# Turning x in full 128-column blocks, with router weights in natural row order loaded behind the gated projection

## What is computed

```python
def rms_norm(x, g):
    y = x * rsqrt(mean(x * x, axis=-1) + EPS)
    return y * g

for i in range(2):
    x = x + mixer_i(rms_norm(x, norm_mix_g[i]))
    h = rms_norm(x, norm_ffn_g[i])
    gl = h @ moe_w_router_group[i]       # (1024, 4)
    el = h @ moe_w_router_expert[i]      # (1024, 4, 8)
    # the best group, its two best experts, their weights "combine"
    x = x + sum_e combine_e * ((silu(h @ w_gate_e) * (h @ w_up_e)) @ w_down_e)
return rms_norm(x, final_norm_g)
```

## Time and profile before

| | |
|---|---|
| median of 3 runs | 815.22 us (815.03 to 815.89) |
| profiled execution, its own time | 816.45 us |
| its span | 814.5 us |
| mean granted TensorE clock | 0.947 |
| TensorE busy / weight loads busy | 711.9 us (87%) / 433.9 us (53%) |
| VectorE / ScalarE / GpSimd busy | 307.8 / 239.5 / 48.8 us |
| transfers | 236.33 MB, 290 GB/s over the span |
| chain that ended last | PE 61%, SP's queue 15%, DMA 11%, ACT 6%, DVE 4% |

### The profile page before, as it was taken

One profiled execution on the slowest core, in us unless ns is written; L12 is line 12 of the kernel. 1 busy time (PEld: TensorE's weight loads), 2 busy tenths in 40 slices (PEclk: granted clock), 3 DMA queues, 4 the chain that ended last, 5 costly groups with the idle time before them and its releaser, 6 DMA issues.

```text
span 814.5 us, 16111 instructions
## 1 busy us (share of the span) xinstructions
PE 711.9 (87%) x6350; PEld 433.9 (53%) x6364; DVE 307.8 (38%) x853; ACT 239.5 (29%) x573; POOL 48.8 (6%) x48
## 2 busy tenths in 40 slices
PE   4999699999997686586999998898999999985994
PEld 4889445557555354254444544465655555652552
DVE  6968991144210011010241535527333443332334
ACT  6672802242111011011312223425222342231224
POOL 3594000000000000000000000000000000000000
PEclk9996899999999798898999999999999999997898
DMA  9630507968999999999990573018899961999981
GB/s 255 173 134 2 208 1 313 408 254 324 421 420 419 420 420 420 422 420 409 381 364 5 210 274 135 1 68 346 350 420 420 422 249 39 423 419 420 422 343 53
DMA packets 59055, 236.33 MB, mean 290 GB/s; under 512 B 19104, under 2 KB 19312, under 8 KB 34416
## 3 DMA queue, kind: packets, MB, share of 16 engines
q1 hardware_dynamic: 58096, 235.23, 73.0%
q10 hardware_dynamic: 896, 0.24, 0.1%
HBM read 234.41 MB, written 1.05 MB: 289 GB/s over the span
## 4 chain that ended last, share of the span: by engine, by line
PE 61%; SPq 15%; DMA 11%; ACT 6%; DVE 4%; issue 2%; DVEq 0%; ACTq 0%
PE ps L1885 11%; SPq L433 10%; PE ps L1976 9%; PE ps L1790 7%; PE ps L1940 6%; SPq L431 4%; DMA ring<-in_moe_w_up 4%; PE ps L1865 4%; DMA hT<-in_moe_w_up 3%; DMA work<-in_moe_w_down 3%; PE ps L1905 3%; PE ps L1661 3%; PE ps L1861 2%; PE ps L2039 2%; PE ps L1708 2%
## 5 line engine op out<-in xcount | busy, mean ns | idle before, releaser
L1885 PE MATMUL ps<-ring,work 128*32 128x256 f32 x1440 | 100.4, 405 | 16.9 <-DMA ring<-in_moe_w_up 12.9
L1885 PE MATMUL ps<-work 128*32 128x256 f32 x848 | 87.4, 433 | 20.7 <-DMA work<-in_moe_w_gate 12.5
L1885 PEld LDWEIGHTS ps<-ring,work 128*32 128x32 f32 x1440 | 57.9, 117 | 53.0 <-issue 30.4
L1976 PE MATMUL ps<-ring,hT 128*128 128x512 f32 x192 | 84.8, 594 | 1.2 <-ACT hT L631 1.2
L1401 DVE TENSOR_TENSOR work<-ps,work 128x256 f32<-128x256 f32 x21 | 12.9, 613 | 188.1 <-PE ps L1885 188.1
L1885 PEld LDWEIGHTS ps<-work 128*32 128x32 f32 x848 | 46.9, 124 | 51.4 <-issue 37.6
L1940 PE MATMUL ps<-ring,work 128*32 128x512 f32 x464 | 58.2, 595 | 1.4 <-DMA ring<-in_moe_w_down 1.1
L1976 PEld LDWEIGHTS ps<-ring,hT 128*128 128x128 f32 x192 | 35.6, 190 | 42.1 <-issue 40.5
L1790 PE MATMUL ps<-ring,work 128*128 128x512 f32 x128 | 55.9, 595 | 0.5 <-ACT work L748 0.5
L1885 PE MATMUL ps<-x,work 128*32 128x256 f32 x160 | 43.3, 432 | 6.3 <-DMA ring<-in_moe_w_up 6.3
L1885 PE MATMUL ps<-hT,work 128*32 128x256 f32 x176 | 44.3, 410 | 0.0
(11 more groups left out here) (334 smaller groups left out, 1121.0 us busy)
## 6 DMA issues: line engine op xcount, KB each, us to landing
ring<-in_moe_w_down SPq DMA_DIRECT2D x21, 2048.0 KB, 22.3
ring<-in_moe_w_gate SPq DMA_DIRECT2D x18, 2048.0 KB, 17.5
ring<-in_moe_w_up SPq DMA_DIRECT2D x17, 2048.0 KB, 29.9
work<-in_moe_w_gate SPq DMA_DIRECT2D x10, 2048.0 KB, 30.9
work<-in_moe_w_up SPq DMA_DIRECT2D x9, 2048.0 KB, 20.9
work<-in_moe_w_down SPq DMA_DIRECT2D x9, 2048.0 KB, 25.3
ring<-in_attn_w_qkv SPq DMA_DIRECT2D x6, 2048.0 KB, 20.4
ring<-in_ssm_w_glu SPq DMA_DIRECT2D x4, 2048.0 KB, 8.5
```

The source lines that it names most:

```text
L1885: ins = mm(ps[s, 6 + j // 2, 0:256], xg[:, k, s], pairs[slots[e // 2]][e % 2][:, k, :], start=(k == 0), stop=(k == KD - 1))
L1976: ins = mm(ps[:, qkv_bank(tt, c), :], hT[:, k, tt * P:(tt + 1) * P], win[slot][:, k, :], start=(k == 0), stop=(k == KD - 1))
```

## The change

Block `k` of hT becomes the 128 adjoining columns 128k to 128k + 127, so that a half of a tile is four full blocks of its own PSUM bank. Router weights and the router's gains (`ffg`, a new tile, for both layers) are loaded in that order. The loads stand behind those of the gated projection, and the copies into hT wait for them, as the first logits and the routing do, with 160 in place of 128. `gq` keeps the gains in (q k) order for the gathered rows of the experts.

```diff
@@ -137,6 +137,7 @@
         rb = sb("rb", [P, 2, NG + E])
+        ffg = sb("ffg", [P, 2, KD])
         small = sb("small", [P, 64])
@@ -413,11 +414,6 @@
             for i, g in ((1, a["norm_ffn_g"][0]), (2, a["norm_mix_g"][1]), (3, a["norm_ffn_g"][1])):
                 sp.dma_start(gq[:, i, :], g.rearrange("(k q) -> q k" if i == 2 else "(q k) -> q k", k=KD)).then_inc(s_gains, 16)
-            for l in range(2):
-                sp.dma_start(wr[:, l, :, 0:NG], a["moe_w_router_group"][l].rearrange("(p k) n -> p k n", k=KD)).then_inc(s_router, 16)
-                sp.dma_start(wr[:, l, :, NG:], a["moe_w_router_expert"][l].rearrange("(p k) g e -> p k (g e)", k=KD)).then_inc(s_router, 16)
-                sp.dma_start(rb[:, l, 0:NG], a["moe_b_router_group"][l].partition_broadcast(P)).then_inc(s_router, 16)
-                sp.dma_start(rb[:, l, NG:], a["moe_b_router_expert"][l].rearrange("g e -> (g e)").partition_broadcast(P)).then_inc(s_router, 16)
@@ -446,6 +442,12 @@
             sp.wait_ge(v_done, 8)
             glu(0, 1)
             glu(1, 1)
+            for l in range(2):
+                sp.dma_start(ffg[:, l, :], a["norm_ffn_g"][l].rearrange("(k q) -> q k", k=KD)).then_inc(s_router, 16)
+                sp.dma_start(wr[:, l, :, 0:NG], a["moe_w_router_group"][l].rearrange("(k p) n -> p k n", k=KD)).then_inc(s_router, 16)
+                sp.dma_start(wr[:, l, :, NG:], a["moe_w_router_expert"][l].rearrange("(k p) g e -> p k (g e)", k=KD)).then_inc(s_router, 16)
+                sp.dma_start(rb[:, l, 0:NG], a["moe_b_router_group"][l].partition_broadcast(P)).then_inc(s_router, 16)
+                sp.dma_start(rb[:, l, NG:], a["moe_b_router_expert"][l].rearrange("g e -> (g e)").partition_broadcast(P)).then_inc(s_router, 16)
@@ -626,10 +628,13 @@
             def keep_tile(i, tt):
 
+                gain = gq[:, 2, :] if i == 2 else ffg[:, i // 2, :]
+                if i == 1 and tt == 0:
+                    act.wait_ge(s_router, 160)
                 act.wait_ge(hT_psum, TURNED[i] + tt)
                 for k in range(4):
                     ins = act.activation(hT[:, k, tt * P:(tt + 1) * P], ps[:, TURN_AT[i][tt], P * k:P * k + P], ACT.Copy,
-                                         scale=gq[:, i, k:k + 1])
+                                         scale=gain[:, k:k + 1])
@@ -1030,9 +1035,12 @@
             def keep_tile(i, tt):
 
+                gain = gq[:, 2, :] if i == 2 else ffg[:, i // 2, :]
+                if i == 1 and tt == 0:
+                    dve.wait_ge(s_router, 160)
                 dve.wait_ge(hT_psum, TURNED[i] + tt)
                 TTo(hT[:, 4:8, tt * P:(tt + 1) * P], ps[:, TURN_AT[i][tt] + 1, :].rearrange("p (k t) -> p k t", k=4),
-                    spread(gq[:, i, 4:8], 2, P), ALU.mult).then_inc(hT_late, 1)
+                    spread(gain[:, 4:8], 2, P), ALU.mult).then_inc(hT_late, 1)
@@ -1616,9 +1620,8 @@
                 pe.wait_ge(mixed, 4 * (i // 2) + 2 * tt + g + 1)
-                rows = slice(64 * g, 64 * g + 64)
-                for k in range(KD):
-                    ins = mm(ps[rows, TURN_AT[i][tt] + k // 4, P * (k % 4):P * (k % 4) + P], by_k(tt)[:, k, rows], ident,
+                for k in range(4 * g, 4 * g + 4):
+                    ins = mm(ps[:, TURN_AT[i][tt] + g, P * (k % 4):P * (k % 4) + P], x[:, tt, P * k:P * k + P], ident,
                              start=True, stop=True)
                 if g:
                     ins.then_inc(hT_psum, 1)
```

More of the change, by code:

```diff
@@ L1268, in moe @@
                 base = 0 if l == 0 else dve.value_load(cum[0][0:1, 2 * NQ:2 * NQ + 1], min_val=1, max_val=MOST)
-                dve.wait_ge(s_router, 128)
+                dve.wait_ge(s_router, 160)
                 dve.wait_ge(logits_done, l + 1)
@@ L1590, in _ @@
             mm = pe.matmul
-            def by_k(tt):
-                return x[:, tt, :].rearrange("p (q k) -> p k q", k=KD)
             def turn():
@@ L1635, in logits @@
                 if tt == 0:
-                    pe.wait_ge(s_router, 128)
+                    pe.wait_ge(s_router, 160)
                 pe.wait_ge(hT_ready, 4 * l + 3 + tt)
```

## The result

| | before | changed |
|---|---|---|
| median | 815.30 us (815.03 to 815.89, 4 runs) | 805.51 us (804.16 to 806.95, 4 runs) |
| ratio, 95% interval | | 0.9879 (0.9859 to 0.9899) |
| profiled execution, its own time | 816.45 us | 804.75 us |
| its span | 814.5 us | 802.8 us |
| mean granted TensorE clock | 0.947 | 0.955 |

The change makes the kernel faster by 9.8 us.

What follows compares the result with a forecast made beforehand. TensorE's chain before each layer's weight stream was taken to bound the kernel; turn savings of 1.90, 1.22, 0.62 and 3.81 summed to 7.55 us, so 815.22 became 807.7 us, range 805.8 to 810.4.

Steps and rivals of the forecast that it cites:

- The bound and the place: Before both layers' expert-weight streams: TensorE's chain sets their start, so what it gains moves each stream as a whole.
- The price of the turn: Turning x into hT: 1.79 us a tile for 3.69, 0.90 a half in a stream, 1.15 after a wait.
- Rival 3: At the turn, a 128-column load costs double: 8 matmuls take 3.69 us again, time stays 815.2; 3 in 100.
- Sum: 1.90 + 1.22 + 0.62 + 3.81 = 7.55 us: Savings: layer 0's tile 0 1.90, tile 1's halves 1.22 and 0.62, layer 1's two turns 3.81.
- the edges of the narrow groups: At the turns: tiling-mode changes that disappear, worth something beside halved work; 1.90 against 1.85 a tile, 1.22 against 1.06.
- Rival 1: Clock dip misses layer 0's gather, 806.0, or a second meets layer 1's gather, 809.3; 10 in 100 each way.
- The loads: Ten router and gain loads behind the gated projection on SP's queue: landed by about 115, needed at 150.7, cost nothing.
- Layer 0's last half: Tile 1, half 1: turn 2.21 to about 1.15 us, but VectorE's copy behind the norm chain limits logits to 0.62 earlier.

Runs made afterwards that it cites:

- the wide kernel with the step: Kernel before, three of its four turns made of 8 matmuls of 128 columns still 8 elements apart: 815.08 us, ratio 0.9994.
- layer 1 alone: Kernel before with the new turn, order and gains in layer 1 only, loads early: 810.79 us, ratio 0.9939.
- The two kernels with halves: Changed kernel, each turned half copied into hT at once: 805.08 us; the same with layer 0's tile 1 logits split around the last half turn: 803.83 us.
- the kernel with the loads late only: Kernel before with only its eight router loads moved behind the gated projection, in their old order: 815.11 us, ratio 0.9995.

## Why the prediction was right and where it was wrong

**The bound and the place: right.** TensorE's chain sets the start of both streams. The first gate projection starts at 183.59 (forecast near 186.5), SP's issue follows at 187.25 (190.1), still 3.66 behind, and the last logits of layer 1 at 542.28 (545.5). SP's issue moved 6.64 and TensorE 6.65, 1.6 us of it the gather and 0.9 the start. Both layers add up. That the stream moves as a whole holds in all 14 profiles: from the first gate projection of layer 0 to the projection behind its long wait it is 183.0 to 183.6 us, with the old turn or a new one.

**The price of the turn: right, for a reason half wrong.** 1.78, 0.89 and 1.79 against 1.79, 0.90 and 1.79; after the wait 1.16 against 1.15. L1612 was the right row, since it has the new turn's form, width and step alike. But the prediction laid the gain to the number of matmuls ("halving alone would save 3.69/2 = 1.85"), from a pitch of about 112 ns in both forms. The pitches are 112 and 115 by chance: twice the columns and no step come out even. Halving alone saves nothing, 3.68 us for 3.69 in the wide kernel with the step. Rival 3 was in truth what the kernel would have done had it kept the step: 815.08.

The prediction also held the rows against a rule. The Trainium skill (TensorE: Matmul & The Clock Gate, LDWEIGHTS) states that a load takes time in proportion to its columns. The rows of before could not test it, as they set a load with the step (211 ns) beside one without (192 ns). At equal step, 64 and 128 columns take 137 and 192 ns, or 211 and 335: the trace agrees with the rule in direction, but the records grow 1.4 and 1.6 times and not twice.

**The step that failed: "Sum: 1.90 + 1.22 + 0.62 + 3.81 = 7.55 us" left out a term, and the range was drawn around it too narrowly.** From the start of the first turn to the start of tile 1's logits, the chain of layer 0 took 25.51 us before and 21.37 after, 4.14 less where the forecast had 1.90 + 1.22 + 0.62 = 3.74. The missing 0.40 is the two projections, 7.06 and 7.08 to 6.87 and 6.88. In layer 1 it is 13.94 and 10.02, 3.92 less for 3.81: 0.19 from the output projection, less 0.08 since the second turn took 1.88 and not 1.79. The sum as measured is 8.06. That is 0.5 of the 2.2 us by which the forecast fell short.

The prediction named the edges of the narrow groups, but looked for them inside the turn's own time, where it took the gap between 1.85 and 1.90 for them. They lie in the neighbours' records. The rule that it named is that of the Trainium skill (TensorEngine Tiling (Array Packing), Key Properties): changing the tiling mode drains the array. The trace fits that rule, as the two projections of 7.06 fall to 6.87 only where the turn's width is theirs, but no record shows a drain as such.

**The other miss: the spread.** The spans of the two profiles differ by 11.7 us: 8.06 of the sum, 0.88 in the start of the first turn, 1.60 in the gather, 0.5 in the transfers of layer 1 up to the end of their long wait, 0.4 behind it (the projection there is 1.25 shorter, and the end of the program gives 0.8 of that back), and 0.2 in small pieces. Rival 1 named the gather alone, put 10 in 100 on its good side, and the range had 0.2 us for the rest. With the 23 runs of before at hand (813.90 to 816.88), a median of four runs needs more room than that. Over the three comparisons the gain is 8.7 to 9.8, and the intervals begin at 8.2, 7.5 and 7.7 us: 8.06 is inside two of them and just below the third. Taken together (9.2, from 8.4 to 10.0) they put it outside, so about 1.1 us beyond the sum is hardly chance. The early start of the first turn, 0.9 us and seen in eight of nine profiles with a new turn, is a candidate for most of it, and the gather for the rest; why it comes with the new turn, and what layer 1 alone gained beyond its 3.9, stays open.

**The loads: right.** They took 18.7 us of the queue for 19 allowed, landed long before the use, and no copy into hT was released by one (all waited for TensorE or for nothing). Moved either way they are worth nothing.

**Layer 0's last half: right.** The logits start 0.62 earlier, limited by VectorE behind the norm chain and not by the turn. The two kernels with halves took that limit away, and their chains are 1.14 and 1.8 us shorter for it.

## What to carry to other kernels

Price a weight load by how its columns lie in memory as well as by their number: compare only rows with the same step, and if a turn reads with a step, change the layout of what is multiplied with it before making the matmuls fewer. When a narrow group of matmuls between wide ones goes, count their effect on the neighbours too, about 0.2 us for each here. And take a range from the spread of many runs: three that agree within 0.9 us hid one of 3 us.

## What the hardware showed that was not expected

- A step of 8 float32 elements between the columns of a weight load made it 1.5 to 1.7 times as long: 137 to 211 ns at 64 columns, 192 to 335 ns at 128. The turn of a tile took 3.7 us with the step at 64 columns and 3.7 to 3.9 at 128.
- A 128 by 512 float32 projection of 16 records was 0.19 us shorter when the matmuls beside it had its own width (6.87 for 7.06), with no instruction of its own changed.
- One kernel's executions differ in the granted clock at places that the program doesn't set: the gather of layer 0 took 3.81 us at a clock of 1.00, or 5.44 with 0.50 in most of it, in two profiles of the same changed kernel. What decides it stays open.
- From 92 to 96 us, TensorE was busy throughout at a clock of 0.53 in one profile of the kernel before, and the start of a turn near 149 us shows it.
- Small loads queued behind 2 MB ones held the issuing queue: one issue of router weights took 7.55 us there and 9.09 in the kernel with the loads late only. At the start of the program none of them took more than 3.62.
